# Two-block transformer in split float32: one 512-column product for the high weights, and another order of casts and subtractions

## The reference

```python
def _conv_ffn(h, w_up, conv_w, w_down):            # first stack, twice
    u = _causal_depthwise_conv(h @ w_up, conv_w)
    gate, val = u[..., :FFN_DIM], u[..., FFN_DIM:]
    return (jax.nn.silu(gate) * val) @ w_down
...
def conv_ffn(h, w_up, ffn_dw_w, ffn_dw_b, w_down):  # second stack, twice
    val, gate = jnp.split(h @ w_up, 2, axis=-1)
    gate = causal_dwconv(gate, ffn_dw_w, ffn_dw_b)
    return (jax.nn.silu(gate) * val) @ w_down
...
    return y @ w_out                                # end of the state-space mixer
```

## Time and profile before

| | us |
|---|---|
| median of 3 runs | 2090.15 (2089.9 to 2092.16) |
| the profiled execution | 2091.13 |
| its span | 2089.3 |
| TensorE products busy | 2068.3 (99%), 16378 products |
| VectorE busy | 1659.0 (79%) |
| ScalarE busy | 1055.8 (51%) |
| GpSimd busy | 257.6 (12%) |
| DMA | 361.95 MB, mean 173 GB/s |

### The profile page before, as it was taken

One profiled execution on the slowest core, in us unless ns is written; L12 is line 12 of the kernel. 1 busy time (PEld: TensorE's weight loads), 2 busy tenths in 40 slices (PEclk: granted clock), 3 DMA queues, 4 the chain that ended last, 5 costly groups with the idle time before them and its releaser, 6 DMA issues.

```text
span 2089.3 us, 38625 instructions
## 1 busy us (share of the span) xinstructions
PE 2068.3 (99%) x16378; PEld 2015.3 (96%) x16378; DVE 1659.0 (79%) x2449; ACT 1055.8 (51%) x1282; POOL 257.6 (12%) x176
## 2 busy tenths in 40 slices
PE   9999999999999999999999999999999999999998
PEld 9999999999999999989999999999988999989998
DVE  8888797787779788798986768767698996758764
ACT  6786354356755434355545445444346445444442
POOL 0212055000006500001201001100000300000100
PEclk9999999999999999999999999999999999999999
DMA  6663455554235455544555435546544555534543
GB/s 262 193 199 125 182 185 184 170 212 150 101 142 182 157 187 202 181 158 162 199 178 174 177 141 182 176 159 212 182 164 150 192 182 182 182 139 167 182 163 118
DMA packets 58300, 361.95 MB, mean 173 GB/s; under 512 B 6736, under 2 KB 9360, under 8 KB 21136
## 3 DMA queue, kind: packets, MB, share of 16 engines
q1 hardware_dynamic: 58128, 359.48, 49.0%
HBM read 358.37 MB, written 1.08 MB: 172 GB/s over the span
## 4 chain that ended last, share of the span: by engine, by line
PE 95%; DVE 2%; ACT 1%; issue 1%; DMA 0%; POOL 0%; SPq 0%; DVEq 0%; ACTq 0%
PE acc L644 79%; PE acc L643 7%; PE acc L759 1%; PE acc L760 1%; PE acc L761 1%; PE acc L964 1%; PE pA L1013 1%; DVE w_lo L1196 0%; DMA raw<-in_wide 0%; PE pC L807 0%; PE pB L1037 0%; PE pD L1124 0%; PE pA L1099 0%; PE pB L1099 0%; PE pB L1124 0%
## 5 line engine op out<-in xcount | busy, mean ns | idle before, releaser
L644 PE MATMUL acc<-in_hi,w_hi 128*128 128x256 f32 x4656 | 1304.9, 285 | 9.8 <-issue 9.4
L644 PE MATMUL acc<-in_hi,w_lo 128*128 128x256 f32 x4656 | 1292.9, 283 | 0.1
L644 PE MATMUL acc<-in_lo,w_hi 128*128 128x256 f32 x4656 | 1230.2, 283 | 0.0
L644 PEld LDWEIGHTS acc<-in_hi,w_hi 128*128 128x128 f32 x4656 | 892.0, 192 | 16.2 <-issue 12.3
L644 PEld LDWEIGHTS acc<-in_hi,w_lo 128*128 128x128 f32 x4656 | 892.1, 192 | 0.6 <-DVE w_lo L1527 0.3
L644 PEld LDWEIGHTS acc<-in_lo,w_hi 128*128 128x128 f32 x4656 | 855.1, 192 | 1.2 <-issue 1.0
L1196 DVE TENSOR_TENSOR w_lo<-raw,w_hi 128x2048 fp32r<-128x2048 f32 (+1 forms) x341 | 737.3, 2164 | 112.7 <-ACT w_hi L2059 111.7
L2059 ACT CAST w_hi<-raw 128x2048 fp32r<-128x2048 f32 (+1 forms) x341 | 614.2, 1804 | 238.5 <-PE acc L644 227.6
L2659 POOL TENSOR_TENSOR in_lo<-arena,in_hi 128x256 fp32r<-128x256 f32 (+1 forms) x112 | 127.2, 1136 | 1212.4 <-ACT in_hi L2519 514.5
L1840 DVE SCALAR_TENSOR_TENSOR arena<-arena,cols 128x256 f32<-128x256 f32 x480 | 200.4, 487 | 0.0
L2669 POOL TENSOR_TENSOR arena<-arena 128x256 f32<-128x256 f32 x44 | 96.3, 2189 | 385.1 <-ACT arena L2341 385.1
(11 more groups left out here) (293 smaller groups left out, 1653.3 us busy)
## 6 DMA issues: line engine op xcount, KB each, us to landing
raw<-in_wide SPq DMA_DIRECT2D x285, 1024.0 KB, 4.8
raw<-in_narrow SPq DMA_DIRECT2D x64, 704.0 KB, 4.1
arena<-cs_rows SPq DMA_DIRECT2D x16, 256.0 KB, 5.0
arena<-in_mem SPq DMA_DIRECT2D x3, 1024.0 KB, 6.9
x<-in_x SPq DMA_DIRECT2D x4, 256.0 KB, 6.1
raw<-in_wide SPq DMA_DIRECT2D x2, 512.0 KB, 5.4
tables<-in_tables SPq DMA_DIRECT2D x1, 1024.0 KB, 17.1
arena<-cs_rows SPq DMA_DIRECT2D x16, 64.0 KB, 5.4
```

What stands on the lines that cost most here:

```text
L644: return mm(outs[m], w[:, k, at], moving[:, c, :], start=start, stop=stop)
```

## The change

1. **Products.** `in_hi` and `in_lo` become the two halves of one tensor `in_both`. In the units for which `side_by_side` holds, the high weights meet both input parts in one product of 512 columns: the left half of the bank collects high by high, the right half high by low. The product low by high goes to the left half, as before with 256 columns. VectorE adds both halves to x, one after the other.
2. **Halves.** No unit is cast and subtracted in halves any more.
3. **Order on VectorE.** `early=True` goes: in ret_q, ret_k and up_b the subtraction for unit u+2 comes ahead of `first(u)`; in `residual` and conv_out only the last unit keeps it behind (`last_first`); the last unit of all other segments has it ahead too. `norm` begins with the subtraction for unit 2, and so does the cross attention. The steps of the angles in the second down segment are at units 0, 2 and 4.
4. **Order on ScalarE.** `norm` has the cast of unit 2 ahead of the root and that of unit 3 ahead of the high parts; the cross attention likewise. Unit 2 of att_o is cast and subtracted ahead of the last two heads, and att_norm(7, 1) comes before att_high(6).

```diff
+        in_both = sb("in_both", [P, 2, IN_CHUNKS, T], F32R)
+        in_hi, in_lo = in_both[:, 0], in_both[:, 1]
...
+        def side_by_side(name, j, units):
+
+            return name == "down" and j < units - 2 or name == "ssm_out" and 2 <= j < units - 1
+
...
+                    if side_by_side(seg.name, j, seg.units):
+                        both = own[:].rearrange("p (a l) -> p a l", a=2)
+                        begins, ends = not (pair and j % 2), not pair or j % 2 == 1
+                        for k in range(nk):
+                            if pair and j % 2 and k == nk - 3:
+                                pe.wait_ge(gin_ready, second_half)
+                            first = seg.chunk0 - (22 if seg.name == "ssm_out" and k >= 14 else 0)
+                            c = first + k + (nk * (j % 2) if pair else 0)
+                            if k or not begins:
+                                product(0, k, lo, in_hi)
+                            last = mm(both, hi[:, k, :], in_both[:, :, c, :], start=k == 0 and begins, stop=k == nk - 1 and ends)
+                            if k == 0 and begins:
+                                product(0, k, lo, in_hi)
...
-                    ahead = (early or (fixed and u == seg.units - 1)) and (
-                        seg.base + j + 2 not in stepped or seg.base + j + 2 in split_behind)
-                    if not ahead and not late:
+                    ahead = last_first and fixed and u == seg.units - 1
+                    mine = not late and seg.base + j + 2 not in elsewhere
+                    if mine and not ahead:
                         split(u + 2, seg, j + 2)
...
-                    if ahead and not late:
+                    if mine and ahead:
                         split(u + 2, seg, j + 2)
                     if second:
                         second(u, j, banks)
...
+                def added(c, out, two):
+
+                    if two:
+                        E.mark(tt(c, out[:, 0:T].unsqueeze(1), c, ALU.add))
+                        E.settle()
+                    return tt(c, out[:, T if two else 0:2 * T if two else T].unsqueeze(1), c, ALU.add)
+
...
                 seg, half = take.next(), NORM_PIECES // 2
+                split(2, seg, 2)
                 reciprocal_std(rstd[:])
-                scaled(name, x, rstd, xn, val_ready, range(DC // 2))
-                split(2, seg, 2)
-                scaled(name, x, rstd, xn, val_ready, range(DC // 2, DC))
+                scaled(name, x, rstd, xn, val_ready)
...
-                    project("up_b", first, second, steps={v_order: 2, silu_ready: 1}, early=True, nth=5 + 3 * l, behind=8)
+                    project("up_b", first, second, steps={v_order: 2, silu_ready: 1}, nth=5 + 3 * l, behind=8, at=7)
...
+                split(2, take.next(), 2)
                 att_low(6)
                 att_low(7)
...
-                        project(n, rotary, lambda u, j, banks: conv_tap(l, u // 2 + o) if j % 2 == 0 else None, early=True)
+                        project(n, rotary, lambda u, j, banks: conv_tap(l, u // 2 + o) if j % 2 == 0 else None)
...
                 seg = take.next()
+                split(2, seg, 2)
                 roots()
-                split(2, seg, 2)
+                split(3, seg, 3)
                 high_parts(xn, chunk0, NORM_PIECES, DC // NORM_PIECES, val_ready)
-                split(3, seg, 3)
```

More of the change, by code:

```diff
@@ L200, in build @@
     base_of = lambda name: [s.base for s in segs if s.name == name]
[L201 to L211, removed]
+    elsewhere = (base_of("att_o")[0] + 2,)
     col, ncol = column_names()
@@ L611, in body @@
                     g = seg.base + j
[L612 to L615, removed]
+                    if g:
                         pe.wait_ge(hi_ready, u + (seg.base + 1))
@@ L644, in product @@
                         return mm(outs[m], w[:, k, at], moving[:, c, :], start=start, stop=stop)
-                    if early == -1 and j == 0:
+                    if side_by_side(seg.name, j, seg.units):
[11 more added lines that the diff above has]
+                                product(0, k, lo, in_hi)
+                    elif early == -1 and j == 0:
                         for m in range(tiles):
@@ L1187, in split @@
                 n = sizes[g]
[L1188 to L1194, removed]
                 dve.wait_ge(hi_ready, u + (seg.base + 1))
@@ L1202, in scale_unit, with project @@
                 tt(bank, bank, rstd[:].unsqueeze(1).broadcast_to([P, 2, T]), ALU.mult).then_inc(early_v, 1)
-            def project(name, first=None, second=None, steps=None, early=False, nth=None, behind=0):
+            def project(name, first=None, second=None, steps=None, last_first=False, nth=None, behind=0, at=6):
                 seg = take(name)
@@ L1231, in body @@
                             split(u + 3, seg, j + 3)
-                        elif u == (7 if early else 6):
+                        elif u == at:
                             split(9, seg, 9)
-                    if ahead and not late:
+                    if mine and ahead:
                         split(u + 2, seg, j + 2)
@@ L1317, in first @@
                             c = x[:, bass.ds(m, 1), :]
-                            out = acc[(seg_base + j // 2 % 2) % 4][:, 0:T].unsqueeze(1)
-                            tt(c, out, c, ALU.add).then_inc(acc_free, 2)
+                            out = acc[(seg_base + j // 2 % 2) % 4]
+                            added(c, out, side_by_side(name, j, last + 1)).then_inc(acc_free, 2)
                     elif kind == "deep":
                         c = x[:, bass.ds(u, 1), :]
-                        tt(c, banks[0].unsqueeze(1), c, ALU.add).then_inc(acc_free, 1)
+                        added(c, acc[(seg_base + u) % 4], side_by_side(name, j, last + 1)).then_inc(acc_free, 1)
                     else:
@@ L1360, in residual @@
                 marks = {"pair": 1 if twice or final else 0.5, "deep": 1, "feat": 2}[kind]
-                seg = project(name, first_and_last, second, steps={v_order: marks}, early=kind == "feat")
+                seg = project(name, first_and_last, second, steps={v_order: marks}, last_first=True)
                 E.passed(sum_ready, 1 + DC)
@@ L1960, in mixed @@
                         tt(y, y, gate[:, bass.ds(u * 2, 2), :], ALU.add).then_inc(val_ready, 1)
-                    project("conv_out", mixed, steps={v_order: 1}, early=True)
+                    project("conv_out", mixed, steps={v_order: 1}, last_first=True)
                     E.passed(inh_ready, 4)
@@ L2004, in run @@
                             x_max(l, u - 2)
-                        split(u + 2, q, u + 2)
+                        if u:
+                            split(u + 2, q, u + 2)
                         if u >= 2:
@@ L2053, in split @@
                     act.wait_ge(unit_done, u + (seg.base - HI + 1))
[L2054 to L2058, removed]
                 copy(w_hi[g % HI][:, 0:n], raw[g % RAW][:, 0:n]).then_inc(hi_ready, 1)
@@ L2083, in body @@
                         return
-                    split(u + 2, seg, j + 2)
+                    if seg.base + j + 2 not in elsewhere:
+                        split(u + 2, seg, j + 2)
                     if use and not (isinstance(u, int) and u < lag):
@@ L2354, in beside @@
                             norm_root()
-                        if layer == 1 and j == 3:
+                        if layer == 1 and j == 5:
                             act.wait_ge(ang_v, 1)
@@ L2604, in run @@
                     q = take("mem_q")
+                    split(2, q, 2)
                     norm_root()
+                    split(3, q, 3)
                     for u in range(4):
-                        split(u + 2, q, u + 2)
+                        if u >= 2:
+                            split(u + 2, q, u + 2)
                         if u >= 2:
```

15 lines of the change are left out of this document (4 added, 11 removed).

## The result

| | us |
|---|---|
| before, median of 4 runs | 2090.66 (2089.90 to 2092.16) |
| after, median of 4 runs | 2104.97 (2104.67 to 2105.91) |
| ratio after to before, 95% interval | 1.0068 (1.0051 to 1.0086) |
| forecast | 2104.0 (2092 to 2114) |

The profiled execution of after took 2105.25 us, 1.75 outside its span. Its page beside the earlier trace rows: head, busy times, the chain's shares, and the two groups of products.

What follows compares the result with a forecast made beforehand. TensorE's nearly gapless products were taken to bound the kernel. Gains of 18.9 us and a loss of 33 in up_b gave 2091.1 - 18.9 + 33 = 2105.2 profiled, 2104 at the median, range 2092 to 2114.

Steps and rivals of the forecast that it cites:

- Part 3, the ring: up_b: VectorE and ScalarE steps wait on each other, 7.04 us per unit against TensorE's 5.76; 16.6 lost per up_b, 33 for two.
- The down pieces: Down units after up_b: turn 5.84 us, down 1 waits 2.0, its last three chunks 1.0, down 2 1.0.
- Rival A: up_b: the loop of waits doesn't bind, as if ScalarE cast u+3 before silu of u; 2071 us, chance 0.09.
- Part 1: Down segments and ssm_out: one 512-column product replaces two of 256 in 696 chunks, 9.3 us saved.
- 0.0133 per chunk: Merged-product chunks: three steps of 0.360 us become two of 0.347 together, taking 0.227 for the 512-column one.
- rival C: Down segments and ssm_out: the merged product saves nothing, perhaps through ramps after width changes; 2113 us, chance 0.09.
- Part 2: Norms, mem_o, att_o, down units, ret_q and ret_k: casts and subtractions moved to where they were late, gains beside the merged product's 9.3.
- The named waits: TensorE waits expected to shrink: norms 5.4 us, att_o 1.3, ret_q and ret_k 1.0, mem_o 0.9, down units 0.6 and 0.4.
- the places of my list: Places with forecast gains from moved steps: norms, mem_o, att_o, down units 1 and 4, ret_q and ret_k.
- x + 0.16: Chain of waits: an "issue" piece of x us was taken to mean x + 0.16 us lost on TensorE.
- no cost: Units formerly in halves: dropping halves costs nothing; att_k and glu first units get whole steps 7.9 us ahead, against 1.9 + 2.3 needed.
- its own range: Whole kernel: the main forecast's range, 2096 to 2112 us, from the up_b loop's bounds and half the gains' uncertainty; chance 0.73.

Runs made afterwards that it cites:

- experiments 5, 7 and 8: After with up_b's old VectorE order, plus: input parts side by side, 2072.16 us; products in blocks of four by width, 2070.48 us; blocks of eight, 2069.32 us.
- the first experiment: After with the old VectorE order in up_b alone (taps of unit u before the subtraction for unit u+2): 2072.10 us, ratio to before 0.9914.
- the fourth experiment: After with up_b's old VectorE order and three 256-column products per chunk everywhere, none merged: 2077.09 us, ratio to before 0.9938.
- the sixth experiment: Before with unit 2 of ssm_out cast and subtracted whole, not in halves: 2088.72 us against 2090.26 beside it, ratio 0.9993.
- the third experiment: Before with only up_b's `early=True` taken away, its first eight units kept as they were: 2119.25 us, ratio to before 1.0138.

## Why the prediction was right, and where it wasn't

**Part 3, the ring, was right in kind and size.** Forecast turn 7.04, measured 7.03; forecast 16.6 us per up_b, measured 202.88 - 186.53 = 16.35, and for both 2104.97 - 2072.10 = 32.9 against 33. The down pieces came too: casts at 1372.07, 1377.89 and 1383.72 in ScalarE's timeline are 5.82 and 5.83 apart (forecast 5.84), and TensorE stands 1.77 us before down 1 (forecast 2.0), 0.78 before its last three chunks, released by GpSimd's low part (1.0), and 1.01 before down 2 (1.0), counted from its starts less a merged product's step of 0.236:

```profile
1381.02 0.36 PE L635 MATMUL acc<-in_both,w_lo 128*128 128x256 f32 x1 [1.62 <-issue]
...
1384.67 0.39 PE L635 MATMUL acc<-in_both,w_lo 128*128 128x256 f32 x1 [0.64 <-POOL in_both L2659]
...
1386.84 0.47 PE L647 MATMUL acc<-in_both,w_hi 128*128 128x512 f32 x1 [0.86 <-ACT w_hi L2054]
```

The place was right as well: before each of units 12 to 21 TensorE stands 1.13 (the first) to 1.21 us, by the starts of its products less a step of 0.12, where "about 1.3" from unit 12 on was forecast. Rival A fell because ScalarE kept its program's order, as the earlier trace rows had it.

**Part 1 was mis-sized.** The term 0.0133 per chunk measured 0.0072. The step that failed is taking 0.227 for the merged product because it was the row of the same type and width: ret_v's products stand in rows of their own width, these alternate. The text had named that as the ground of rival C and then taken the end where it costs nothing. The truth lies between, at 54% of the saving: of the some 7 ns that are missing, some 4 go with the changes of width and some 3 with the merged product itself (experiments 5, 7 and 8). The second additions cost nothing that could be seen.

**Part 2 was too low by some 3 us, and that hid the first miss: luck.** Forecast without the merged product 9.6, measured 13.0 at the medians. The named waits went as forecast: in the first experiment's chain the norm is solid, and in the chain of after at ret_q one piece stands where the earlier trace rows had two with 0.36 between them:

```profile
859.93 20.16 PE acc L635 x168
```

At att_o TensorE's waits (each the step between two starts less 0.12), from 560 to 605 us in before and from 555 to 600 in after, fell from 3.42 to 2.19, 1.2 won against 1.3. Chain of waits there:

```profile
592.43 2.29 DVE w_lo L1187
594.73 0.68 DVE x L1324 x2
...
598.48 0.37 DVE in_both L1274
598.89 4.60 PE acc L635 x36
```

Beside the earlier trace rows the products go on at 598.89 instead of 604.18 (most of these 5.3 us were won before att_o); what is late is still x and the last input part, as the step said. Before and the kernel of the fourth experiment make the same 16378 products, so that the start times can be subtracted one by one. In these two traces the places of my list brought 11.4 us against 9.6: the norms 5.90 (forecast 5.4), mem_o 1.03 (0.9), att_o 1.32 (1.3), down unit 1 0.78 (0.6), down unit 4 0.72 (0.4), around ret_q and ret_k 1.63 (1.0). Part of this is that behind each wait the next few steps are longer too, some 0.06 us together, which x + 0.16 leaves out. Not in my list were 0.30 in up_a, 0.2 in the first 90 us, and 2.44 in ssm_out, of which 1.45 is a clock that fell in before's profiled execution (last section). Without these 1.45 the two traces differ by 12.9, close to the 13.0 of the medians. I had looked at the steps that the diff names as moved and not at the `stepped` unit of ssm_out, which I priced as "no cost" without asking for a gain.

**The sum.** 2105.2 against 2105.25 in the measure of the profiled execution is closer than its terms: -4.3 in part 1 and +3.4 in part 2 nearly cancel, and the ring's 33 measured 32.9. The sign, and its place, rested on the ring alone. One bound in the text doesn't follow from its working: a ring of 6.6 us costs 11 per up_b, 22 in place of 33 for two, which gives 2104 - 11 = 2093 and not 2096 as the lower end of "its own range".

## What to carry to other kernels

Before you move a step on one engine, close the loop through the other engines' programs: add up every link that waits for the one before, per unit, and compare with TensorE's time per unit. A subtraction that is moved ahead to be early is late when what it waits for (here the cast) itself stands behind the work that it was moved past (here the taps, through silu and hidden cast). Where a product of one width is to stand among products of another, price it from a row with the same neighbours, and if there is none, keep equal widths together.

## What the runs showed of the chip that I had not expected

**Half subtractions beside GpSimd.** In before the third unit of ssm_out is subtracted in halves while GpSimd makes the last low parts, on which TensorE waits. VectorE in before:

```profile
198.41 1.64 DVE L1191 TENSOR_TENSOR w_lo<-raw,w_hi 128x1024 fp32r<-128x1024 f32 x1 [1.37 <-ACT w_hi L2056]
199.97 2.28 DVE L1193 TENSOR_TENSOR w_lo<-raw,w_hi 128x1024 fp32r<-128x1024 f32 x1
```

GpSimd's four operations, in before, in the sixth experiment (whole unit) and in after:

```profile
L2702 POOL TENSOR_TENSOR in_lo<-arena,in_hi x4: 1294/1298/2239, 195.1 to 198.9; 128x512 fp32r<-128x512 f32 x4
```

```profile
L2702 POOL TENSOR_TENSOR in_lo<-arena,in_hi x4: 1267/1302/1306, 195.8 to 199.6; 128x512 fp32r<-128x512 f32 x4
```

```profile
L2702 POOL TENSOR_TENSOR in_both<-arena,in_both x4: 1298/1311/1333, 195.8 to 199.5; 128x512 fp32r<-128x512 f32 x4
```

Columns are shortest, median and longest, then first and last start. In before the last one, from 198.9 on, begins beside VectorE's first half and takes 2.24 instead of 1.30; VectorE's second half, begun beside it, takes 2.28 where the same operation takes 1.22 at 593.50, with GpSimd idle. With a whole unit VectorE begins at 199.9, during GpSimd's last operation, is the one that is held (3.08 instead of 2.29), and GpSimd isn't. TensorE's wait is 0.98 us longer with the halves (starts 1.98 apart against 1.00), in both kernels with them (before and the third experiment) and in none of the eight without. The Trainium skill (GPSIMD Engine Reference, "1. Specifications") says that GpSimd shares its SBUF interfaces with VectorE, and that operations of VectorE with two SBUF inputs contend; these have two, and the trace agrees.

**The granted clock behind it.** Busy times from 200 to 203 and 203 to 206 us (PE, PEld, DVE, ACT, POOL, clock, DMA, GB/s), in before, then in the third experiment with the same wait:

```profile
200.00:203.00 3.00, 1.78 (x10) 1.78 (x11) 2.93 (x4) 1.19 (x1) 1.16 (x1) 0.78 0.19 22
203.00:206.00 3.00, 3.00 (x19) 3.00 (x19) 2.96 (x4) 0.71 (x1) 0.00 (x0) 0.65 0.80 330
```

```profile
200.00:203.00 3.00, 2.03 (x17) 2.04 (x18) 2.93 (x4) 1.44 (x1) 0.91 (x1) 1.00 0.35 44
203.00:206.00 3.00, 3.00 (x28) 3.00 (x27) 2.97 (x4) 2.03 (x2) 0.00 (x0) 1.00 0.83 328
```

Before's profiled execution fell to the 1.2 GHz level (products 0.21 us apart instead of 0.12) after TensorE had stood for 1.98 us, and lost 1.45 us more; the third experiment's stood just as long and kept 2.4 GHz. So the expectation of the sixth experiment, that the longer wait cost the clock, isn't shown: such a wait doesn't always do it. Of the 3.0 us by which after is shorter here, 1.45 is not the kernel's in every execution, 0.98 is the wait, and the rest is the merged products. At the medians the whole unit brought 1.5 us, between the 0.98 of the wait and the 2.44 of both, but the interval leaves open whether it brought any. The two profiled executions don't add to it: they are 1.14 us apart (2091.13 and 2089.99), since that of the sixth experiment won 2.44 here and lost 0.7 between 98 and 128 us and 0.4 at the very end, which its edit doesn't touch.
